# Last down group by token halves, raw h turned for w_in, its norm applied in w_in's evacuations

## The reference, cut to what matters

```
x = x + g2 * rms_norm(sqrelu_mlp(modulate(rms_norm(x, ng2), sh2, sc2), w_mlp_in, w_mlp_out), ng3)
h = x
xn = rms_norm(h, attn_norm_g)                       # h * rsqrt(mean(h*h) + eps) * gain
gq, gk, gv, gg, ga, fq, fk, fv, fg, ff, mq, mg = split(xn @ w_in)
log_a = log_sigmoid(ga @ gla_a_w2 + gla_a_b) / 16   # decays of the gated linear attention
o = concat(gla(gq, gk, gv, log_a), fox(fq, fk, fv, ff), memory(mq, mem))
h = h + (rms_norm(o) * concat(silu(gg), sigmoid(fg), sigmoid(mg))) @ w_out
```

## Time and profile before

| | |
|---|---|
| median of 3 runs | 2237.3 us (2237.26 to 2237.48) |
| profiled execution | 2241.01 us, of which the span is 2239.3 us |
| PE busy | 2149.7 us (96%) |
| DVE busy | 1337.1 us (60%) |
| ACT busy | 973.6 us (43%) |
| chain that ended last | PE 88%, DVE 6%, DMA 4%, ACT 2%, issue 1% |
| mean granted TensorE clock | 0.977 of full |

### The profile page before, as it was taken

How to read it: one execution, slowest core, us unless ns; L and a number is a source line. 1 busy time by engine, 2 the same in 40 slices (tenths; PEclk the granted TensorE clock), 3 DMA queues, 4 the chain that set the end, 5 groups by cost and what they waited for, 6 DMA issues and landing times.

```text
span 2239.3 us, 31205 instructions
## 1 busy us (share of the span) xinstructions
PE 2149.7 (96%) x11689; PEld 1823.6 (81%) x11689; DVE 1337.1 (60%) x1317; ACT 973.6 (43%) x1133; POOL 45.1 (2%) x69
## 2 busy tenths in 40 slices
PE   5988988999999999997999999999999999999999
PEld 4756867888888888886989879888888888888887
DVE  5578976655656555656667545656555554655563
ACT  4233435343434344443533447744434343443342
POOL 0000000000000000001000000000000000000000
PEclk9899989999999999999999989999999999999999
DMA  9998996677667667666455435556666666656664
GB/s 358 337 381 317 389 377 203 211 220 215 206 216 214 214 209 219 204 221 207 143 169 142 141 95 144 194 188 182 193 191 188 187 195 188 187 188 193 184 192 152
DMA packets 219187, 478.97 MB, mean 214 GB/s; under 512 B 14708, under 2 KB 15084, under 8 KB 218336
## 3 DMA queue, kind: packets, MB, share of 16 engines
q1 hardware_dynamic: 211940, 450.98, 62.8%
q0 software_dynamic: 6480, 25.69, 3.7%
q10 hardware_dynamic: 684, 1.14, 0.1%
HBM read 472.50 MB, written 5.24 MB: 213 GB/s over the span
## 4 chain that ended last, share of the span: by engine, by line
PE 88%; DVE 6%; DMA 4%; ACT 2%; issue 1%; SPq 0%; DVEq 0%; ACTq 0%
PE ps L439 21%; PE ps L457 13%; PE ps L458 13%; PE ps L459 13%; PE ps L440 11%; PE ps L443 3%; PE ps L444 3%; PE ps L445 3%; DMA raw<-in_w_mod_dram 2%; DVE acc L1240 2%; PE ps L483 1%; DMA raw<-in_w_in_dram 1%; PE ps L529 1%; DMA slot<-in_norm_g_dram 1%; DVE wl L1215 1%
## 5 line engine op out<-in xcount | busy, mean ns | idle before, releaser
L1215 DVE TENSOR_TENSOR wl<-raw,wh 128x1024 fp32r<-128x1024 f32 x688 | 811.6, 1220 | 352.7 <-ACT wh L884 351.6
L884 ACT ACTIVATE wh<-raw 128x1024 fp32r<-128x1024 f32 x688 | 700.6, 1054 | 550.0 <-DMA raw<-in_w_down_dram 161.7
L439 PE MATMUL ps<-xt,wh 128*128 128x512 f32 x2048 | 724.9, 399 | 9.0 <-DVE wl L1215 9.0
L440 PE MATMUL ps<-xt,wl 128*128 128x256 f32 x2048 | 575.6, 281 | 0.0
L439 PEld LDWEIGHTS ps<-xt,wh 128*128 128x128 f32 x2048 | 386.3, 189 | 106.2 <-issue 10.7
L457 PE MATMUL ps<-wh,u 128*128 128x512 f32 x1152 | 449.3, 390 | 0.0
L458 PE MATMUL ps<-wl,u 128*128 128x512 f32 x1152 | 448.2, 389 | 0.0
L459 PE MATMUL ps<-wh,u 128*128 128x512 f32 x1152 | 448.2, 389 | 0.0
L440 PEld LDWEIGHTS ps<-xt,wl 128*128 128x128 f32 x2048 | 388.3, 190 | 0.3
L457 PEld LDWEIGHTS ps<-wh,u 128*128 128x128 f32 x1152 | 216.2, 188 | 45.5 <-issue 0.5
L459 PEld LDWEIGHTS ps<-wh,u 128*128 128x128 f32 x1152 | 216.2, 188 | 45.0
(11 more groups left out here) (266 smaller groups left out, 1507.7 us busy)
## 6 DMA issues: line engine op xcount, KB each, us to landing
raw<-in_w_mod_dram SPq DMA_DIRECT2D x160, 512.0 KB, 7.6
raw<-in_w_mlp_in_dram SPq DMA_DIRECT2D x128, 512.0 KB, 3.7
raw<-in_w_mlp_out_dram SPq DMA_DIRECT2D x128, 512.0 KB, 4.7
raw<-in_w_up_dram SPq DMA_DIRECT2D x128, 512.0 KB, 3.8
raw<-in_w_down_dram SPq DMA_DIRECT2D x128, 512.0 KB, 3.7
raw<-in_w_in_dram SPq DMA_DIRECT2D x96, 512.0 KB, 3.7
raw<-in_fnet_w_out_dram SPq DMA_DIRECT2D x32, 512.0 KB, 5.9
slot<-in_w_mod_dram POOLq DMA_DIRECT2D x32, 512.0 KB, 4.5
```

The costliest lines, as they stand in the source:

```text
L439: mm(o, a, flat(xt[:, kt, :, :]), start=first, stop=end, skip_group_check=True)
L440: last = mm(o[:, 0:S], b, xt[:, kt, 0, :], start=False, stop=end, skip_group_check=True)
L884: A(flat(wh[:, i, :, :]), raw[:, landed[0], :], ACT.Copy).then_inc(sem("w_hi"), 1)
L1215: V.tensor_tensor(flat(wl[:, s, :, :]), raw[:, s, :], flat(wh[:, i, :, :]).bitcast(F32), ALU.subtract).then_inc(sem("w_lo"), 1)
```

## The change

- The last down group runs all eight chunks for token half 0, then all eight for half 1 (`down_by_halves`). `chunk_used` is counted in the second pass. The gate rows stand after chunk 1 of the first pass.
- Half 0 is added, squared, gated, reduced and made into h (four pieces of 512 columns) while half 1 is multiplied; two rounds of its transposes stand before half 1's last chunk. Half 1 follows when the group ends.
- h is turned raw, by transposes with the identity (`raw_turn`), in four rounds in banks `RAW_TURN = (6, 2, 4, 6)`; rounds 2 and 3 stand after chunks 1 and 2 of w_in's group 0. Its gain is applied as before in the copies (`raw_hi`, `raw_lo`), the root is not.
- The root's mean, `root(7)` and `diagonals` are done during group 0. `norm_row` multiplies ones by the diagonals, which gives the roots as a row in every partition (`rbc`). w_in's evacuations multiply by that row, or for gv and fv, whose rows are tokens, by `rstd` per partition.
- `att_narrow` moves behind chunk 6 of group 0, `att_la` behind chunk 7. The splits of group 0 are written out one by one among the pieces of h; those of group 1's chunks 0 to 3 stand behind the evacuation of the narrow projection.
- The gates get a VectorE pass `normed(zt, ps)` first; ScalarE's Abs and the later products read `zt` in SBUF. The bank is free after this pass.
- The gate's first half (`gate(1, ..., (0,))`) stands before the split of chunk 6 of the last down group, the second half and the products in `gate_rest`.
- h is spilled by GpSimd when all twelve pieces are there (8 pieces, 4 of them of this h, before).

```diff
+                def down_by_halves():
+                    G = G0 + QT * 2 * GQ - 1
+                    pe.wait_ge(sem("evacuated"), G - 1)
+                    for half in range(HALVES):
+                        for i in range(CH):
+                            if half == 0:
+                                pe.wait_ge(sem("w_lo"), CH * G + i + 1)
+                            o = ps[:, 4 * (G % 2) + half, :]
+                            for kt in (2 * i, 2 * i + 1):
+                                hi, lo = (u[:, kt, z, half * P:(half + 1) * P] for z in range(2))
+                                mm(o, hi, wh[:, i, kt % 2, :], start=kt == 0, stop=False, skip_group_check=True)
+                                mm(o, hi, wl[:, i, kt % 2, :], start=False, stop=False, skip_group_check=True)
+                                done = mm(o, lo, wh[:, i, kt % 2, :], start=False, stop=kt == KT - 1, skip_group_check=True)
+                            if half == 1:
+                                done.then_inc(sem("chunk_used"), 1)
+                            elif i == CH - 1:
+                                done.then_inc(sem("half_mm"), 1)
+                            if (half, i) == (0, 1):
+                                between()
+                            if (half, i) == (1, CH - 2):
+                                raw_turn(0, 0)
+                                raw_turn(1, 0)
...
+            def raw_turn(r, half):
+                pe.wait_ge(sem("h_piece"), 4 + 4 * half + r + 1)
+                if r == 3:
+                    pe.wait_ge(sem("xt_ready"), 8 + 2)
+                for j in range(4):
+                    kt = 4 * r + j
+                    last = nc.tensor.transpose(ps[:, RAW_TURN[r] + j // 2, (j % 2) * S + half * P:(j % 2) * S + (half + 1) * P],
+                                               h[:, half, kt * P:(kt + 1) * P], ident[:, :])
+                if half == 1:
+                    last.then_inc(sem("turned"), 1)
...
-            transposes(2, h)
+            raw_turn(0, 1)
+            raw_turn(1, 1)
+            def norm_row():
+                pe.wait_ge(sem("dg_ready"), 6)
+                for half in range(HALVES):
+                    last = mm(ps[:, 5, half * P:(half + 1) * P], ones[:, :], dg[:, half, :], start=True, stop=True)
+                last.then_inc(sem("row_mm"), 1)
...
-                    if (k, i) == (0, 1):
+                    if k == 0 and i in (1, 2):
+                        for half in range(HALVES):
+                            raw_turn(i + 1, half)
+                    if (k, i) == (0, 6):
+                        norm_row()
                         att_narrow()
-                    if (k, i) == (0, 5):
+                    if (k, i) == (0, 7):
                         att_la()
...
+            last_squares(0)
             root(5)
+            hi_static(CH * G_WIN)
+            hi_static(CH * G_WIN + 1)
+            h_squares(4, (0, 1), 2)
+            last_squares(1)
             root(6)
+            raw_hi(0, (0, 1))
+            raw_hi(0, (2, 3))
+            hi_static(CH * G_WIN + 2)
+            raw_hi(1)
+            hi_static(CH * G_WIN + 3)
+            hi_static(CH * G_WIN + 4)
+            raw_hi(2)
+            hi_static(CH * G_WIN + 5)
+            raw_hi(3)
+            h_squares(4, (2, 3), 2)
+            hi_static(CH * G_WIN + 6)
+            root(7)
+            hi_static(CH * G_WIN + 7)
...
+            mean(4, 5, "ysq", 8 * QT - 1, slice(0, 1), gate_rest)
+            dve.wait_ge(sem("y_gated"), 4)
+            for r in range(4):
+                raw_residual(0, r)
+            lo_static(CH * G_WIN)
+            lo_static(CH * G_WIN + 1)
+            summed_half(1)
+            mean(4, 6, "ysq", 8 * QT, slice(1, 2))
+            raw_residual(1, 0)
+            raw_residual(1, 1)
+            raw_lo(0, (0, 1), 1)
+            raw_lo(0, (2, 3), 2)
...
+            def normed(dst, src, by=1.0):
+                t = src.rearrange("p b (t n) -> p (b t) n", n=S)
+                return V.scalar_tensor_tensor(out=dst, in0=t, scalar=by, in1=rbc[:, :].rearrange("p (o n) -> p o n", o=1)
+                                              .to_broadcast([P, 4, S]), op0=ALU.mult, op1=ALU.mult)
...
-                        act.wait_ge(sem("chunk_used"), CH * G + CH)
-                        A(flat(gt[:, :, :]).rearrange("p (b n) -> p b n", b=2), ps[:, 2 * (G % 2):2 * (G % 2) + 2, :],
-                          ACT.Abs).then_inc(sem("gate_abs"), 1)
+                        act.wait_ge(sem("evacuated"), G + 1)
+                        A(gt[:, :, :], zt[:, :, :], ACT.Abs).then_inc(sem("gate_abs"), 1)
...
+                    if j == 0:
+                        dve.wait_ge(sem("chunk_used"), CH * G + CH)
+                        normed(zt[:, :, :], src).then_inc(sem("evacuated"), 1)
```

More of the change, by code:

```diff
@@ L683, in quarter @@
                             for e in range(2):
-                                down(q, p, e, last=p == 1 and e == 1)
+                                if p == 1 and e == 1:
+                                    down_by_halves()
+                                else:
+                                    down(q, p, e)
                     else:
@@ L1077, in down @@
                         hi_run(m0)
-                    if ups == 0:
+                    if ups == 0 and not final:
                         act.wait_ge(sem("evacuated"), q * 8 + p * 2 + (G0 + 4 + e + 1))
@@ L1087, in mlp_quarter @@
                         for e in range(2):
-                            down(p, e, final=ups > 0 and p == 1 and e == 1)
+                            down(p, e, final=p == 1 and e == 1)
                 else:
@@ L1154, in _ @@
                 G = G_WIN + k
[L1155 removed]
+                if k == 0:
+                    for i in range(4):
+                        hi_static(CH * (G + 1) + i)
+                else:
+                    hi_run(CH * G + 4, gate_steps(k - 1) if k >= 9 else None)
                 if k == 0:
@@ L1529, in down @@
                             lo(4 + j, 4 + j, m0 + (j + 1))
+                    elif tail:
+                        for j in range(4):
+                            if j == 2:
+                                gate(1, (2, 6), 2 + MODN, (0,))
+                            lo(4 + j, 4 + j, m0 + (j + 1))
+                        return
                     else:
-                        lo_run(m0, gate_and_products if tail else None)
+                        lo_run(m0)
                     if early and e == 0:
@@ L1585, in _, with gate_rest @@
             mlp_quarter(G_ML1, 0, QT - 1, True, y, last=True)
-            dve.wait_ge(sem("ysq"), 8 * QT)
-            gated(GQ - 1)
-            mean(4, 5, "ysq", 8 * QT)
-            dve.wait_ge(sem("y_gated"), GQ)
-            for n in range(4):
-                residual(n)
-            mean(2, 6, "hsq", 8)
+            for g in range(2):
+                dve.wait_ge(sem("ysq"), 8 * (QT - 1) + 2 * (g + 1))
+                gated(g)
+            summed_half(0)
+            def gate_rest():
+                gate(1, (2, 6), 2 + MODN, (1,))
+                dve.wait_ge(sem("ysq"), 8 * (QT - 1) + 6)
+                gated(2)
+                dve.wait_ge(sem("ysq"), 8 * QT - 1)
+                gated(3, slice(0, 1))
@@ L1593, in _ @@
+            raw_residual(1, 2)
+            raw_lo(1, n=3)
+            gated(3, slice(1, 2))
+            lo_static(CH * G_WIN + 3)
+            dve.wait_ge(sem("y_gated"), 5)
+            raw_residual(1, 3)
+            lo_static(CH * G_WIN + 4)
+            raw_lo(2, n=4)
+            lo_static(CH * G_WIN + 5)
+            raw_lo(3, n=5)
+            lo_static(CH * G_WIN + 6)
+            mean(2, 7, "hsq", 8)
             diagonals()
-            for r in range(4):
-                xt_lo_round(2, r, v("attn", KT))
+            lo_static(CH * G_WIN + 7)
```

121 lines of the change are left out of this document (78 added, 43 removed).

## The result

The changed kernel takes 2242.2 us (median of 20 runs, 2237.4 to 2248.1), the kernel before 2238.3 in the same session (20 runs, 2233.0 to 2242.3). The ratio is 1.0018, with a 95% interval of 1.001 to 1.0025: 3.9 us slower, between 2 and 6.

A forecast was written before the change was run, and what follows sets the result against it. TensorE was taken to bound the kernel, with a 24.2 us seam. -17.7 + 2.7 + 4.15 + 1.1 + 3.9 + 2.8 + 7.0 = +4.0, added to the median, gave 2241.3 us, range 2231 to 2247.

The forecast's parts named there:

- The seam, -17.7: Between last down group and w_in: w_in's first matmul starts at 1055.2 instead of 1072.94, 17.7 us earlier.
- the half order: Last down group by token halves: hides 7.3 us of half 0's VectorE work; rival that it does nothing, 2248.6, chance 0.05.
- Added in group 0, +2.7: w_in's group 0: 16 transposes 2.0 us, two switches 0.2 and two row matmuls 0.5 are added.
- the new seam's clock, +2.2: Behind the new seam: TensorE's clock falls after 5.3 us with 1 us of work, costing 2.2 us.
- The wait in group 1, +4.15: Mid group 1: TensorE waits 4.15 us on a VectorE split behind the later decay chain; rival of no wait, 2235.0, chance 0.14.
- The clock fall behind it: Behind the wait in group 1: TensorE's clock falls, costing 2.2 us.
- The gates, 1.1, 0, 3.9, 2.8: Groups 8, 9, 10, 11: a VectorE pass ahead of Abs delays readers by 1.1, 0, 3.9 and 2.8 us.
- the sign that I had named, one wait above 4: Group 10, at L787: its wait would grow from 1.4 us to above 4.
- The rival in which these passes are hidden: Groups 8, 10 and 11: gate passes do not move the step chains, so 2230.9 us; chance 0.17.
- The clock, +7.0: Clock falls: 2.2 at new seam, 2.2 in group 1, 2.0 ahead of L787, 0.6 group 11; between 3.5 and 10 us.
- The 0.6 at w_out: Group 11's wait: a clock fall, less likely than not after 1.9 us in one piece, counted at 0.6 us.
- behind group 1 the rest keeps its distances: Behind group 1: VectorE waits for TensorE again, so no further change was counted there.

The follow-up runs named there:

- Run ten: Changed kernel with the half order undone: last down group goes through its chunks once, both halves per chunk, half 0's turns behind the group; 2249.1 us, ratio 1.0048.
- Run five: Kernel before with only the decay product att_la moved from behind chunk 5 to behind chunk 7 of group 0; 2242.3 us, ratio 1.0025.
- run six: Changed kernel with four wide matmuls on constants, read by nobody, filling TensorE's wait ahead of chunk 4 of group 1; 2242.0 us, ratio 1.002.
- Run four: Kernel before with only a VectorE copy of the gates' banks to SBUF ahead of Abs, groups 8 to 11; 2250.2 us, ratio 1.0051.
- run one: Changed kernel with group 10's gate pass moved into a gap of the memory softmax and group 11's ahead of the memory head root wait; 2234.6 us, ratio 0.9982.
- run two: Changed kernel with narrow projection and norm row behind chunk 4, att_la behind chunk 5 of group 0, and related splits earlier; 2239.2 us, ratio 1.0003.
- seven: Changed kernel with 26 transposes of the identity filling TensorE's wait ahead of chunk 4 of group 1; 2240.5 us, ratio 1.0011.
- three: Changed kernel with gate passes and decay chain both moved earlier, and pt copied ahead of u's low part in groups 8 and 10; 2226.2 us, ratio 0.9942.
- eight: The kernel of run three with 24 transposes of the identity, read by nobody, in the seam's idle 3.1 us; 2225.1 us, ratio 0.9937.
- nine: The kernel of run eight with the odd level's steps ahead of the split of chunk 3 of the next group, on ScalarE and VectorE; 2216.5 us, ratio 0.9901.

## Why the prediction was right

It said 2241.3 and the kernel takes 2242.2. Point by point, from the profiled execution, in which the terms add up to its 5.7 us:

- **The seam, -17.7.** w_in's first matmul at 1055.27 against 1055.2 counted. Reckoned from the start of the down group (1022.90, before 1023.38) the lead is 17.2. Run ten confirms the size of the half order (8.3 against 7.3: two splits, 2.35 us, stand ahead of half 1's evacuation when both halves come at once).
- **Added in group 0, +2.7, and the new seam's clock, +2.2.** Group 1 begins 12.9 us earlier, so the two together are 4.8. Behind the seam 29 matmuls start 0.21 us apart instead of 0.12, which is 2.7; that leaves 2.1 for what was added. Each was about half a us off, one up and one down.
- **The wait in group 1, +4.15.** 3.89. Run five shows the larger part by itself. The clock fall behind it was put at 2.2; from group 1's start to group 2's the lead falls from 12.9 to 7.4, by 5.5, of which 1.6 is not the wait, and run six gives 1.2 for the four chunks alone.
- **The gates, 1.1, 0, 3.9, 2.8.** L833 waits 1.08 in group 8; in group 10 the waits of 0.69, 0.37 and 3.60 replace 1.39, +3.9 at the same reader (the sign that I had named, one wait above 4, did not come, because two chunks ahead of it took a part); w_out's group 0 loses 2.8. Run four shows the same waits in the old kernel, run one takes most of them away. The rival in which these passes are hidden fell; run one is what it would have looked like.
- **The clock, +7.0.** 7.1 at the places I had named: the 2.7 in group 0, the 1.6 above, and 2.8 instead of 2.0 at L833, where TensorE runs at 0.50 over 1424 to 1428. The 0.6 at w_out did not come. That the total agrees so well is luck, since one wait brings different falls. At the same wait of 3.6 us ahead of the memory product (L833, L788 in run four) the low stretch lasts 6.8 us in the changed kernel and run two and 3.4 in runs six, seven and ten, and run four has none.
- **Not counted: +2.5 in groups 2 to 6.** 0.8 us more of level waits and a clock fall of 1.7 near 1171. I had written that behind group 1 the rest keeps its distances. That step failed, by an amount that the range covered. The 0.8 fits the instruction fetch of runs six and seven. The clock fall stays open: it came near there in the changed kernel and in runs one, six and seven, earlier in runs two and three, and not in the kernel before or runs four, five, eight and nine. It is no fixed cost of the change either, since run ten has the changed kernel's code there and no fall. Each of these falls begins 0.6 to 1.4 us behind the end of a level wait of 1.8 us or more, but others as long brought none (2.8 us in run one).

In the profile the sum is thus -17.7 + 4.8 + 3.9 + 1.6 + 2.5 + 1.1 + 3.9 + 2.8 + 2.8 = +5.7. The runs say 3.9 with an uncertainty of about 2. That the median met the forecast to 1 us is therefore partly luck: the terms were each within 1 us, one of 2.5 was missing, and one execution stands some us off the median. What the runs do show is that the large terms are real: the half order undone costs 7.0 us, and the gate passes moved return 6.8.

## What to carry to other kernels

A shorter seam is worth its length only if the chains behind it keep ahead of their readers: before moving a product later, count the reader's lead behind it, in chunks, against the follower's whole serial chain. A pass put ahead of a gate costs its place in an in-order queue rather than its length: place it in a gap where the engine waits for another one anyway. And work that is needed only a group later (here one split, behind a transfer) shall not stand ahead of work that TensorE asks for next; that reorder was worth 0.26% by itself.

## What the runs showed of the hardware

- Instruction fetches go on during the run: 59 on queue 8 with 0.97 MB, so 16 KB each, one every 11 to 26 us in this stretch. They belong to TensorE's list as far as runs six and seven tell, since a change of that list alone moved one. The 512 KB load that one meets lands 0.8 to 1.6 us late; that the two share a DMA engine is likely and not shown. Whether this reaches TensorE depends on where the fetch falls: 36 instructions more, in dead matmuls of about the same length, moved the total level waits from 7.0 to 5.8 us. So an instruction added or removed ahead of a tight stretch can change the waits in it.
- A wait of TensorE filled with transposes of a constant kept the granted clock at 1.00 over the seam (run eight) and over group 1 (run seven), and left the following start where it was. In group 1, with wide matmuls as fill, this is 1.2 us by the trace, too little for these medians.
- One wait does not always bring the same fall of the clock. At 3.6 us ahead of the memory product six traces have low stretches of 6.8, 6.8, 3.4, 3.4, 3.4 and 0 us; at 3.9 us in group 1 three traces have 3.4, 6.8 and 6.8.
